# FFN modulation vectors: the spreading sum as two rounded products, with three of eight terms and the remainder on POOL

## The reference

```python
c_act = silu(c)
for i in range(2):
    mod = c_act @ ada_w[i] + ada_b[i]          # ada_w: 1024 x 9216
    sh1, sc1, gt1, sh2, sc2, gt2, sh3, sc3, gt3 = split(mod, 9)
    h = h + 0.5 * gt1 * swiglu(modulate(h, sh1, sc1), w_gu[i, 0], w_down[i, 0])
    h = h + gt2 * mixer(modulate(h, sh2, sc2))
    h = h + 0.5 * gt3 * swiglu(modulate(h, sh3, sc3), w_gu[i, 1], w_down[i, 1])
```

## Time and profile before

| what | value |
|---|---|
| time of three runs | 1547.06, 1551.1, 1552.14 us |
| median | 1551.1 us |
| lowest run | 1547.06 us |
| span of the profiled execution | 1547.0 us |
| busy share of PE, DVE, ACT, POOL | 83%, 62%, 34%, 5% |
| mean granted TensorE clock | 0.852 |
| chain that ended last, share of PE, DVE, ACT, DMA | 73%, 17%, 4%, 4% |

### The profile page before, as it was taken

How to read it: one execution, slowest core, us unless ns; L and a number is a source line. 1 busy time by engine, 2 the same in 40 slices (tenths; PEclk the granted TensorE clock), 3 DMA queues, 4 the chain that set the end, 5 groups by cost and what they waited for, 6 DMA issues and landing times.

```text
span 1547.0 us, 16841 instructions
## 1 busy us (share of the span) xinstructions
PE 1284.6 (83%) x6354; PEld 1027.9 (66%) x6354; DVE 963.1 (62%) x1240; ACT 527.6 (34%) x693; POOL 76.9 (5%) x66
## 2 busy tenths in 40 slices
PE   1699998874988999988999947777654995899997
PEld 0477886763556778866888834576654994688885
DVE  5687885786446878868776355446592438644543
ACT  1444332434324443334344234334321002334331
POOL 1000000000000000000000000005170004000000
PEclk9999999696568999998999977888665555899999
DMA  7688874550015888867886432410102011464541
GB/s 263 228 291 304 303 269 157 206 198 18 1 55 179 295 305 304 275 212 243 279 284 214 127 89 89 150 61 1 28 1 55 2 56 55 145 208 163 194 159 55
DMA packets 186520, 252.19 MB, mean 163 GB/s; under 512 B 31508, under 2 KB 122644, under 8 KB 186456
## 3 DMA queue, kind: packets, MB, share of 16 engines
q1 hardware_dynamic: 147216, 175.74, 34.1%
q10 hardware_dynamic: 39240, 75.58, 14.3%
HBM read 249.19 MB, written 2.10 MB: 162 GB/s over the span
## 4 chain that ended last, share of the span: by engine, by line
PE 73%; DVE 17%; ACT 4%; DMA 4%; issue 2%; SPq 1%; ACTq 0%; DVEq 0%; POOL 0%; POOLq 0%
PE bank L624 18%; PE bank L626 18%; PE bank L625 18%; DVE inv_tmp L1538 2%; DVE ada_acc L1359 2%; PE bank L611 2%; PE bank L752 2%; DMA raw<-in_rwkv_w_rkv_dram 1%; PE bank L967 1%; DVE gu_lo L1368 1%; PE bank L975 1%; DVE xn L1411 1%; PE bank L643 1%; PE bank L762 1%; DVE inv_out L1540 1%
## 5 line engine op out<-in xcount | busy, mean ns | idle before, releaser
L624 PE MATMUL bank<-gu_hi,xT_hi 128*128 128x512 f32 (+1 forms) x880 | 352.3, 400 | 17.5 <-ACT z L1103 8.4
L625 PE MATMUL bank<-gu_lo,xT_hi 128*128 128x512 f32 (+1 forms) x880 | 350.3, 398 | 0.0
L626 PE MATMUL bank<-gu_hi,xT_lo 128*128 128x512 f32 (+1 forms) x880 | 350.1, 398 | 0.0
L1368 DVE TENSOR_TENSOR gu_lo<-raw,gu_hi 128x2048 fp32r<-128x2048 f32 (+1 forms) x116 | 257.2, 2256 | 80.8 <-ACT gu_hi L1042 80.5
L1042 ACT CAST gu_hi<-raw 128x2048 fp32r<-128x2048 f32 (+1 forms) x116 | 213.1, 1882 | 81.0 <-PE bank L626 28.6
L624 PEld LDWEIGHTS bank<-gu_hi,xT_hi 128*128 128x128 f32 x880 | 172.0, 195 | 57.4 <-ACT z L1103 9.3
L1359 DVE SCALAR_TENSOR_TENSOR ada_acc<-ada_raw,cact,ada_acc 128x512 f32<-128x512 f32 x252 | 189.4, 752 | 14.4 <-DMA ada_raw<-in_ada_w_dram 1.7
L625 PEld LDWEIGHTS bank<-gu_lo,xT_hi 128*128 128x128 f32 x880 | 171.8, 195 | 37.4 <-issue 0.5
L626 PEld LDWEIGHTS bank<-gu_hi,xT_lo 128*128 128x128 f32 x880 | 171.2, 195 | 35.8
L1374 DVE TENSOR_TENSOR dn_lo<-raw,dn_hi 128x2048 fp32r<-128x2048 f32 x44 | 100.9, 2292 | 127.9 <-ACT dn_hi L1049 127.9
L624 PE MATMUL bank<-dn_hi,hT_hi 128*128 128x512 f32 x352 | 156.4, 444 | 17.9 <-DVE dn_lo L1374 17.9
(11 more groups left out here) (235 smaller groups left out, 1538.3 us busy)
## 6 DMA issues: line engine op xcount, KB each, us to landing
raw<-in_ffn_w_gu_dram SPq DMA_DIRECT2D x176, 512.0 KB, 6.3
ada_raw<-in_ada_w_dram ACTq DMA_DIRECT2D x144, 512.0 KB, 5.1
raw<-in_ffn_w_down_dram SPq DMA_DIRECT2D x44, 1024.0 KB, 6.8
raw<-in_rwkv_w_rkv_dram SPq DMA_DIRECT2D x24, 512.0 KB, 5.5
raw<-in_dsa_w_in_dram SPq DMA_DIRECT2D x16, 512.0 KB, 5.3
raw<-in_dsa_w_out_dram SPq DMA_DIRECT2D x8, 512.0 KB, 4.9
out_raw<-in_rwkv_w_out_dram SPq DMA_DIRECT2D x4, 512.0 KB, 5.3
raw<-in_rwkv_w_out_dram SPq DMA_DIRECT2D x4, 512.0 KB, 5.4
```

Source lines behind the costliest of these rows:

```text
L624: nc.tensor.matmul(out_ap, sta_hi, mov_hi, start=start, stop=False, skip_group_check=True)
L625: nc.tensor.matmul(out_ap, sta_hi, mov_lo, start=False, stop=False, skip_group_check=True)
L626: return nc.tensor.matmul(out_ap, sta_lo, mov_hi, start=False, stop=stop, skip_group_check=True)
L1368: nc.vector.tensor_tensor(gu_lo[:, par, ks, 0:width], buf[:, i, 0:4 * width].rearrange("p (k c) -> p k c", k=4), gu_hi[:, par, ks, 0:width ...
```

## The change

For the 29 vectors that the FFNs make (not for the 7 others):

- POOL makes the terms k = 0, 1, 2: for each a multiplication of `ada_raw[k]` by the column `cact[k]`, broadcast, and an add, the first one with the bias row. The result is `ada_part`. Each instruction waits for the one before it.
- DVE makes only k = 3 to 7 and starts from `ada_part` (`ada_rest`).
- ACT rounds the sum to fp32r, `acc_hi` (`round_acc`); it stands behind `load_ada` and ahead of `round_block`.
- POOL subtracts: `acc_lo = ada_acc − acc_hi` (`pool_rest`).
- PE spreads the sum with two fp32r products by a rounded matrix of ones, `acc_hi` and `acc_lo` (`ffn_ada_total`), at the place where L611 stood. It waits for `acc_ready`, which `pool_rest` raises.

```diff
+    ADA_POOL0 = (0, NB, 2 * NB, 2 * NB + 7)
+    ON_POOL = 3
...
+            def ada_ffn(f):
+
+                v0, nv = ADA_FFN[f]
+                u0 = ADA_POOL0[f]
+
+                def step(b, odd, ada):
+                    v, u = v0 + b, u0 + b
+                    peeled = isinstance(b, int)
+                    if ada:
+                        pool.wait_ge(bias_in, 16 * v + 16)
+                        if not (peeled and b == 0):
+                            pool.wait_ge(ada_step, v * KD - (KD - ON_POOL) + 1)
+                        for k in range(ON_POOL):
+                            if k % 2 == 0:
+                                pool.wait_ge(ada_in[k // 2], 16 * v + 16)
+                            term = ada_term if k else ada_part
+                            if k:
+                                pool.wait_ge(ada_part_step, u * 2 * ON_POOL + 2 * k)
+                            nc.gpsimd.tensor_tensor(term[:], ada_raw[:, k // 2, k % 2, :],
+                                                    cact[:, k:k + 1].broadcast_to([P, HALF]), ALU.mult).then_inc(ada_part_step, 1)
+                            pool.wait_ge(ada_part_step, u * 2 * ON_POOL + 2 * k + 1)
+                            nc.gpsimd.tensor_tensor(ada_part[:], ada_part[:], term[:] if k else ada_bias[:], ALU.add
+                                                    ).then_inc(ada_part_step, 1)
+                    if nv and not (peeled and (b == 0 or b > nv)):
+                        pool_rest(u - 1)
+
+                run_blocks(pool, f, step)
+                if nv == NB:
+                    pool_rest(u0 + NB - 1)
+
+            def pool_rest(u):
+
+                pool.wait_ge(acc_hi_ready, u + 1)
+                nc.gpsimd.tensor_tensor(acc_lo[:], ada_acc[:], acc_hi[:].bitcast(F32), ALU.subtract).then_inc(acc_ready, 1)
+
+            ada_ffn(0)
             causal(relu_used, (2, 6), score, NEG, score_masked)
             causal(offset_ready, (1, 2), offset, HIDDEN, offset_masked)
+            ada_ffn(1)
+            ada_ffn(2)
...
+            def ffn_ada_total(v, u, spread):
+
+                pe.wait_ge(acc_ready, u + 1)
+                nc.tensor.matmul(spread[:], ones_r[:], acc_hi[:], start=True, stop=False)
+                nc.tensor.matmul(spread[:], ones_r[:], acc_lo[:], start=False, stop=True).then_inc(ada_sum, 1)
...
                         if nv and not (peeled and b > nv):
                             pe.wait_ge(hT_ready[0], ub)
-                            ada_total(v0 + b - 1, TB[0])
+                            ffn_ada_total(v0 + b - 1, ADA_POOL0[f] + b - 1, TB[0])
                         down(ub - 1, 0, peeled and b == 1, False)
...
+            def round_acc(v):
+                act.wait_ge(ada_step, v * KD + KD)
+                nc.scalar.copy(acc_hi[:], ada_acc[:]).then_inc(acc_hi_ready, 1)
...
                     if ada:
                         load_ada(v0 + b, v0 // HV, v0 % HV + b)
+                    if nv and not (peeled and (b == 0 or b > nv)):
+                        round_acc(v0 + b - 1)
                     if not (peeled and b == NB - 1):
                         round_block(n + 1, (n0 + odd + 1) % 2, peeled and n == 0)
...
+            def ada_rest(v, u):
+
+                dve.wait_ge(ada_part_step, u * 2 * ON_POOL + 2 * ON_POOL)
+                dve.wait_ge(ada_sum, v)
+                for k in range(ON_POOL, KD):
+                    if k % 2 == 0 or k == ON_POOL:
+                        dve.wait_ge(ada_in[k // 2], 16 * v + 16)
+                    if k > ON_POOL:
+                        dve.wait_ge(ada_step, v * KD + k)
+                    ins = nc.vector.scalar_tensor_tensor(out=ada_acc[:], in0=ada_raw[:, k // 2, k % 2, :],
+                                                         scalar=cact[:, k:k + 1],
+                                                         in1=ada_acc[:] if k > ON_POOL else ada_part[:],
+                                                         op0=ALU.mult, op1=ALU.add)
+                    ins.then_inc(ada_step, 1 if k > ON_POOL else ON_POOL + 1)
...
                     if ada:
-                        ada_products(v0 + b)
+                        ada_rest(v0 + b, ADA_POOL0[f] + b)
```

More of the change, by code:

```diff
@@ L112, in trunk @@
         chunk_decay = place("chunk_decay", [P, KD, NC])
+        ones_r = place("ones_r", [P, P], F32R, at=top["at"])
         rstat = place("rstat", [P, 128])
@@ L188, in trunk @@
         gn_sq = place("gn_sq", [P, HALF], at=r0 + 16384 + 2048)
+        ada_part = place("ada_part", [P, HALF], at=spare_at)
+        ada_term = place("ada_term", [P, HALF], at=spare_at + 2048)
+        acc_hi = place("acc_hi", [P, HALF], F32R, at=spare_at + 4096)
+        acc_lo = place("acc_lo", [P, HALF], F32R, at=spare_at + 6144)
         z_small = place("z_small", [P, TT, DSA_SMALL], at=spare_at)
@@ L215, in trunk @@
         ada_step = sem("ada_step")
+        ada_part_step = sem("ada_part_step")
+        ada_part_made = sem("ada_part_made")
+        acc_hi_ready = sem("acc_hi_ready")
+        acc_ready = sem("acc_ready")
+        ones_ready = sem("ones_ready")
         ada_sum = sem("ada_sum")
@@ L692, in ffn @@
                 if nv == NB:
-                    ada_total(v0 + NB - 1, TB[0])
+                    ffn_ada_total(v0 + NB - 1, ADA_POOL0[f] + NB - 1, TB[0])
             def dsa(q):
@@ L1005, in _ @@
             pe.wait_ge(consts, 4)
+            pe.wait_ge(ones_ready, 1)
             for v in range(ADA_FRONT):
@@ L1318, in ffn @@
                 if nv == NB:
+                    round_acc(v0 + NB - 1)
                     copy_mods(v0 + NB - 1, v0 % HV + NB - 1, TB[0])
@@ L1323, in _ @@
             act.wait_ge(consts, 4)
+            nc.scalar.copy(ones_r[:], ones[:]).then_inc(ones_ready, 1)
             for v in range(ADA_FRONT):
```

## The result

| what | before | after |
|---|---|---|
| median (runs) | 1551.62 us (4) | 1897.5 us (4) |
| lowest and highest | 1547.06, 1553.49 us | 1895.18, 1901.22 us |
| ratio after / before, with its 95% interval | | 1.2236 [1.2212, 1.226] |
| span of the profiled execution | 1547.0 us | 1895.4 us |
| mean granted TensorE clock | 0.852 | 0.800 |

The forecast was 1898 us. The total came out within 1 us of it; not every term did.

What follows compares the result with a forecast made beforehand. TensorE alone was taken to bound the blocks (busy 17.80 of 17.80 us). 26 × (11.5 stall + 2.3 restart) less 12 gave +347 us, 1894 against the profiled span, plus 4.1 for the median: 1898 us, range 1785 to 2005.

Steps and rivals of the forecast that it cites:

- The queue order: In POOL's queue, six new-vector instructions stand ahead of the old acc_lo, so TensorE waits at the sum in 26 blocks.
- The landing: The new vector's first piece lands 3.6 us after issue, at T+4.8; T is the start of a block's gate-up.
- The turns: POOL and DVE's gu_lo shut each other out for whole instructions; acc_lo ready at T+17.4, TensorE stalled 11.5 us a block.
- the rival at the low end: POOL and DVE miss each other, no turns with gu_lo: stall 7.1 us, total 1770 us; chance 0.12.
- The clock: After each stall TensorE restarts at half speed for 3.6 to 6.1 us, losing 2.3 us a block.
- The two rounded products: At TensorE's modulation sum, two rounded products replace the f32 one: 0.40 us less for each of 29 vectors, −12 us.
- The sum: 26 blocks times stall plus restart (11.5 + 2.3) give 359 us, less 12: +347 us.
- high end: Rival that POOL is slower yet, 1.65 us an instruction: stall 15.5 us, restart 3.0, total 2020 us; chance 0.10.
- The cover on DVE: DVE loses 2.3 us of products a block but had 3.8 us to spare, so this is worth nothing.
- the clock came back inside the block: Answers the rival that TensorE's clock stays low all block: 39.4 us a block, total 2113 us; chance 0.06.
- nothing else hid the wait: Answers the rival of no stall at TensorE's sum, only the 0.40 us a vector gained: 1539 us; chance 0.03.

Runs made afterwards that it cites:

- run with fillers: The changed kernel plus 46 extra rounded 512-column products, results thrown away, on TensorE ahead of each wait for acc_ready in vector-making blocks: 1855.89 us, ratio 1.1937.
- late sum: The changed kernel with TensorE's two summing products moved behind gate-up of half 1, POOL's queue as it was: 1706.11 us, ratio 1.0992.
- one term: The changed kernel with ON_POOL = 1 in place of 3: POOL makes one multiplication and one add, DVE seven products; 1781.2 us, ratio 1.1449.
- earlier load: The changed kernel with ACT's load of the new vector issued first in its block's program, ahead of silu and round_down: 1717.26 us, ratio 1.1054.

## Why the prediction was right, step by step

- **The queue order** carried it, and held: 26 waits as counted, all for `acc_lo`, in the blocks named. Moving the remainder ahead of the six took the waits from 303.2 to 39.0 us.
- **The landing** came at T+5.2, not T+4.8: 4.0 us from issue instead of 3.6. TensorE came at T+6.1 instead of T+5.9.
- **The turns**: forecast T+17.4 for the remainder, measured T+17.7, so a stall of 11.7 instead of 11.5 us. The way there was a little different. Alone POOL takes 1.04 and 1.26 us (taken from the rows: 1.0 and 1.2; the estimate from the Trainium skill, GPSIMD Engine Reference, "Elementwise — side-by-side cycle accounting", was 1.12 for an add, and the rows were nearer), and two of its instructions took turns, as in the table, but right behind each other. Without turns the wait is 7.7 us, so the rival at the low end was priced about right (7.1 us); it did not happen, because `gu_lo` started 0.6 us behind POOL's first instruction.
- **Two blocks without `gu_lo`** were overlooked: block 10 of FFN 0 and of FFN 1 waits 7.6 and 7.5 us, 8 us less together. The first waiting block of each FFN waited 13.5, 14.2 and 14.5 us, 7 us more together. So 26 × 11.5 = 299 stood for 303.2.
- **The clock**: taken 2.3 us a block, 60 us. The run with fillers gives 1.8, 47 us in all; this term was mis-sized by 13 us. The two gaps in the rows of before gave 3.6 and 6.1 us at low clock, and I took the middle; behind the 26 waits it was 2.8 to 6.2 us, 3.9 on average.
- **The two rounded products**: taken −0.40 us a vector, measured −0.43.
- **The sum**: forecast 299 + 60 − 12 = 347 us. Measured are waits 303, restarts 47 and products −12, which give 338 us, and the span grew by 348. Some 10 us are in no term, and they made up for the oversized restart: that the total is right to 1 us is partly luck. By stage the run with fillers puts a restart at 1.3 us in FFN 0 and at 2.0 us in FFN 1 and FFN 2. Waits, these restarts and −0.43 us a vector then give +123 for FFN 0 (measured +124.0), +131 for FFN 1 (+135.7) and +83 for FFN 2 (+86.0). The blocks of FFN 1 and 2 take 31.2 and 31.4 us on average instead of 30.8 with the same waits; with the fillers they take 29.3 and 29.7 against 29.5 in FFN 0. So most of what they take longer is a dearer restart; why it is dearer there, and the 9 us left in the three stages, was not followed.
- **Small slips in the working**: the low and the high end count 0.5 us for the steps from one instruction to the next, where the chain counts 7 × 0.1 = 0.7. By the estimate of 1.12 us from the Trainium skill (GPSIMD Engine Reference, the section named above) the four adds would be 0.3 us shorter together, not about 0.5, and the total 8 us lower, not 12. Neither changes the forecast.
- **The cover on DVE** ("3.8 us to spare, worth nothing") was true for the work taken off, but the prediction did not ask what happens when DVE has to wait for POOL. Behind a stalled TensorE it costs nothing; with the order mended the ring of POOL, DVE and ACT takes 19.5 us and costs 2 us a block.
- **Rivals**: the clock came back inside the block after each of the 26 waits, within 6.2 us, POOL was no slower than its turns, and nothing else hid the wait.

## What to carry to other kernels

When an idle engine takes over part of a loop's work, write its queue down and look for an old result that stands behind inputs of the next round: here two lines in the wrong order cost 296 of 346 us. An "idle" engine is also a link: what DVE had done by itself now waits for a load, for POOL and for turns, and one more hand-over used up the slack of the engine behind it. Once engines wait for each other in a ring, add up the time once round it; when it is longer than the busiest engine's block, it sets the pace. And try each part of a compound change alone: the rounded sum was a small gain, hidden under the move to POOL.

## What the runs showed of the hardware that was not expected

- **A shorter wait did not cost less clock.** How long TensorE worked at the lower level behind the start of its sum, as the mean over the waits of a kernel, with the shortest and longest: 4.2 us (3.4 to 6.0) after the 24 waits of 1.9 to 4.3 us with the late sum; 5.0 us (2.9 to 6.2) after the 24 waits of 6.4 to 9.6 us with one term; 4.3 us (3.6 to 5.8) after 7.4 to 10.6 us with `gu_lo` held back; 5.0 us (2.9 to 6.1) after 9.3 to 15.4 us with the earlier load; 3.9 us (2.8 to 6.2) in the changed kernel, where 24 of the 26 waits are 11.2 to 14.5 us. The spread within a kernel is larger than that between kernels, and no order by length shows. One block says little here.
- **POOL and DVE's two-input instructions in turns**: alone and beside `gu_lo`, 1.26 becomes 3.19 and 1.04 becomes 2.97 us for POOL, 4.50 becomes 5.88 for two `gu_lo`. A POOL instruction that meets a running `gu_lo` is longer by 1.9 us, nearly the 2.25 us of one half of `gu_lo`, so the number of turns counts more than the number of POOL's instructions: taking four of seven away left both turns in place.
- **A wait can alternate**: with the earlier load, every second block waited for 9 to 10 us, since a block without a wait frees the pieces' buffer later, measured against the next sum.
